# Cross-attention in another order: head 0's scores inside the query product, turning and values alternating with scores

## What is computed

```python
def mem_cross_attn(h, mem, w_q, w_kv, w_o):
    q = _heads(h @ w_q, XA_HEADS).astype(F32)
    k, v = jnp.split(mem @ w_kv, 2, axis=-1)
    k = _heads(k, XA_HEADS).astype(F32)
    v = _heads(v, XA_HEADS).astype(F32)
    p = jax.nn.softmax(jnp.einsum('bhtd,bhmd->bhtm', q, k) * (XA_HD ** -0.5), axis=-1)
    o = jnp.einsum('bhtm,bhmd->bhtd', p, v).astype(h.dtype)
    return _merge(o) @ w_o
...
h = layer_norm(DN_ALPHA * h + mem_cross_attn(...), ln_g[layer, 1], ln_b[layer, 1])
```

## Time and profile before

| | |
|---|---|
| median of 3 runs | 2856.29 us (2851.35 to 2857.38) |
| profiled execution, its own time | 2854.78 us |
| its span, first to last instruction | 2853.1 us |
| mean granted clock of TensorE | 0.965 |
| TensorE busy | 2600.0 us, 91% |
| VectorE busy | 1352.4 us, 47% |
| ScalarE busy | 1072.4 us, 38% |
| share of TensorE in the chain that ended last | 72% |

### The profile page before, as it was taken

One profiled execution on the slowest core, in us unless ns is written; L12 is line 12 of the kernel. 1 busy time (PEld: TensorE's weight loads), 2 busy tenths in 40 slices (PEclk: granted clock), 3 DMA queues, 4 the chain that ended last, 5 costly groups with the idle time before them and its releaser, 6 DMA issues.

```text
span 2853.1 us, 35119 instructions
## 1 busy us (share of the span) xinstructions
PE 2600.0 (91%) x13316; PEld 2107.0 (74%) x13316; DVE 1352.4 (47%) x1869; ACT 1072.4 (38%) x1569; POOL 206.3 (7%) x249
## 2 busy tenths in 40 slices
PE   6978789788999988988899999999997888999999
PEld 5855578567887877776468888888875666788887
DVE  5764377567764355423554333235525544433323
ACT  2235422223454134434644333234424554433322
POOL 1101111001000010000201000001001111100000
PEclk8989989899999999999999999999989999999999
DMA  7730174424323222221012222323310000223232
GB/s 247 265 117 1 47 249 147 162 73 163 118 89 110 96 62 74 88 74 59 1 38 89 89 90 93 103 89 105 104 55 15 22 15 7 67 90 102 90 100 83
DMA packets 178691, 263.21 MB, mean 92 GB/s; under 512 B 8232, under 2 KB 127904, under 8 KB 178592
## 3 DMA queue, kind: packets, MB, share of 16 engines
q1 hardware_dynamic: 156608, 194.00, 20.9%
q0 software_dynamic: 15232, 58.72, 5.9%
q10 hardware_dynamic: 6752, 9.09, 0.9%
HBM read 255.51 MB, written 2.10 MB: 90 GB/s over the span
## 4 chain that ended last, share of the span: by engine, by line
PE 72%; DVE 12%; ACT 7%; issue 5%; POOL 3%; DMA 1%; DVEq 0%; ACTq 0%; SPq 0%; POOLq 0%
PE ps L689 20%; PE ps L691 19%; PE ps L690 19%; PE ps L1281 2%; DVE wlo L2087 2%; PE ps L916 2%; ACT decay L1875 1%; PE ps L958 1%; DVE macc L2104 1%; PE ps L1386 1%; ACT pnt_h L1986 1%; DVE pnt_l L2091 1%; DVE nst L2608 1%; POOL diag L2867 1%; PE ps L1201 1%
## 5 line engine op out<-in xcount | busy, mean ns | idle before, releaser
L2087 DVE TENSOR_TENSOR wlo<-raw,whi 128x2048 fp32r<-128x2048 f32 x180 | 412.1, 2290 | 729.2 <-ACT whi L1506 729.0
L689 PE MATMUL ps<-acth,wlo 128*128 128x512 f32 (+1 forms) x1888 | 703.4, 373 | 24.1 <-DVE actl L2091 12.6
L691 PE MATMUL ps<-acth,whi 128*128 128x512 f32 (+1 forms) x1888 | 696.6, 369 | 0.0
L690 PE MATMUL ps<-actl,whi 128*128 128x512 f32 (+1 forms) x1888 | 696.5, 369 | 0.0
L1506 ACT ACTIVATE whi<-raw 128x2048 fp32r<-128x2048 f32 x180 | 343.6, 1910 | 585.5 <-PE ps L691 585.5
L689 PEld LDWEIGHTS ps<-acth,wlo 128*128 128x128 f32 x1888 | 358.1, 190 | 87.9 <-DVE actl L2091 15.1
L690 PEld LDWEIGHTS ps<-actl,whi 128*128 128x128 f32 x1888 | 358.1, 190 | 60.1 <-issue 1.2
L691 PEld LDWEIGHTS ps<-acth,whi 128*128 128x128 f32 x1888 | 357.4, 189 | 59.8
L689 PE MATMUL ps<-whi,hid_l 128*128 128x512 f32 x528 | 207.9, 394 | 5.2 <-DVE conv_t L2315 3.4
L690 PE MATMUL ps<-wlo,hid_h 128*128 128x512 f32 x528 | 206.2, 390 | 0.0
L691 PE MATMUL ps<-whi,hid_h 128*128 128x512 f32 x528 | 206.0, 390 | 0.0
(11 more groups left out here) (329 smaller groups left out, 3690.9 us busy)
## 6 DMA issues: line engine op xcount, KB each, us to landing
mraw<-in_mod_w POOLq DMA_DIRECT2D x48, 1024.0 KB, 5.5
raw<-in_ffn_w_in SPq DMA_DIRECT2D x44, 1024.0 KB, 4.9
raw<-in_ffn_up SPq DMA_DIRECT2D x22, 1024.0 KB, 4.9
raw<-in_ssm_w_in SPq DMA_DIRECT2D x20, 1024.0 KB, 5.1
raw<-in_ffn_w_out SPq DMA_DIRECT2D x20, 1024.0 KB, 4.9
raw<-in_sb_win SPq DMA_DIRECT2D x12, 1024.0 KB, 5.0
raw<-in_ffn_down SPq DMA_DIRECT2D x10, 1024.0 KB, 4.9
raw<-in_xa_wkv SPq DMA_DIRECT2D x8, 1024.0 KB, 5.1
```

The costliest lines, as they stand in the source:

```text
L689: nc.tensor.matmul(o, ll, rh, start=start, stop=False, skip_group_check=True)
L690: nc.tensor.matmul(o, lh, rl, start=False, stop=False, skip_group_check=True)
L691: return nc.tensor.matmul(o, lh, rh, start=False, stop=stop, skip_group_check=True)
L2087: nc.vector.tensor_tensor(wlo[:, slot, :], raw[:, slot, :], whi[:, slot, :].bitcast(F32), ALU.subtract) \
```

## The change

Head 0's scores are issued inside the second query pair, behind its first two banks, into banks 4 and 5. ACT makes head 0's exponentials right after the split of slot 0, ahead of the copies of query banks 2 and 3; DVE makes head 0's maxima after that split and normalises after the second two modulation units, ahead of the split of slot 1. The pair is written out instead of being a loop of one turn.

In `cross_attention`, `banks_out` and `turns_out` no longer stand in front. Scores of head 1 wait for banks 2 and 3 one by one, and the wait for the modulation store (`turns_out`) stands before the values of head 0. The order on TensorE becomes: turning 0, scores 1, values 0, scores 2, turning 1, scores 3, turning 2, values 1, turning 3, values 2, values 3. The score banks of the heads are 4, 2, 0 and 2. `pxt` has two buffers, the second where the memory input lay. ACT and DVE have orders of their own to match. The output product waits for `heads_free` 4 before its first unit and 8 before its second, in place of 8 before both.

```diff
@@ -317,7 +317,7 @@
     vx = place("vx", [P, MB, D], at=o); o += 8192
     qx = place("qx", [P, KC, SEQ], at=o); o += 16384
     px = place("px", [P, 2, TB, MEM], at=o); o += 8192
-    pxt = place("pxt", [P, MB, SEQ], at=o); o += 4096
+    pxt = [place("pxt0", [P, MB, SEQ], at=o), place("pxt1", [P, MB, SEQ], at=ARENA)]; o += 4096
     o = ARENA
@@ -360,6 +360,8 @@
     w2k = place("w2k", [P, 2, 2, HD], at=WIDE + 7168)
     cst2 = place("cst2", [P, 4, TB * 4 * QG], at=WIDE + 7168)
     kcmp = place("kcmp", [P, KV, CMP], at=SUFFIX)
+    SCORE_BANK = (4, 2, 0, 2)
     T_STRIPS = {3: 0, 2: 512, 0: 896, 1: 1024}
@@ -1023,46 +1025,61 @@
             pe.wait_ge(o_free, 2 + KC)
             turns(o_free, KC)
+        def head_scores(hd):
+            if hd == 0:
+                pe.wait_ge(turned_free, turns.seen["turned_free"] + 4)
+            for t in range(TB):
+                bank = SCORE_BANK[hd] + t // 2
+                if t % 2 == 0:
+                    if hd == 1:
+                        pe.wait_ge(bank_free, turns.seen["bank_free"] + bank + 1)
+                    if hd == 3:
+                        pe.wait_ge(probs, 8)
+                for c in range(2):
+                    last = nc.tensor.matmul(ps[:, bank, MEM * (t % 2):MEM * (t % 2) + MEM],
+                                            qx[:, 2 * hd + c, P * t:P * t + P], kx[:, 2 * hd + c, :],
+                                            start=t % 2 == 0 and c == 0, stop=c == 1, skip_group_check=True)
+                if t % 2:
+                    last.then_inc(scores, 1)
+        def head_turn(hd):
+            pe.wait_ge(probs_normed, hd + 1)
+            if hd:
+                pe.wait_ge(probs_copied, 2 * hd)
+            for m in range(MB):
+                for t in range(TB):
+                    last = nc.tensor.transpose(ps[:, 4 + m, P * t:P * t + P], px[:, hd % 2, t, P * m:P * m + P],
+                                               ident[:])
+                last.then_inc(probs_turned, 1)
+        def head_values(hd):
+            pe.wait_ge(probs_copied, 2 * hd + 2)
+            if hd == 0:
+                turns_out()
+            for c in range(2):
+                if hd:
+                    pe.wait_ge(heads_free, 2 * hd - 1 + c)
+                for m in range(MB):
+                    last = nc.tensor.matmul(ps[:, 6 + c, :], vx[:, m, 256 * hd + P * c:256 * hd + P * c + P],
+                                            pxt[hd % 2][:, m, :], start=m == 0, stop=m == MB - 1)
+                last.then_inc(heads_out, 1)
         def cross_attention():
-            banks_out()
-            turns_out()
-            def head_scores(hd):
-                for t in range(TB):
-                    bank = 2 * (hd % 2) + t // 2
-                    if t % 2 == 0 and hd >= 2:
-                        pe.wait_ge(probs, 4 * (hd - 1))
-                    for c in range(2):
-                        last = nc.tensor.matmul(ps[:, bank, MEM * (t % 2):MEM * (t % 2) + MEM],
-                                                qx[:, 2 * hd + c, P * t:P * t + P], kx[:, 2 * hd + c, :],
-                                                start=t % 2 == 0 and c == 0, stop=c == 1, skip_group_check=True)
-                    if t % 2:
-                        last.then_inc(scores, 1)
-            head_scores(0)
-            for hd in range(XA_HEADS):
-                if hd + 1 < XA_HEADS:
-                    head_scores(hd + 1)
-                pe.wait_ge(probs_normed, hd + 1)
-                if hd:
-                    pe.wait_ge(probs_copied, 2 * hd)
-                for m in range(MB):
-                    for t in range(TB):
-                        last = nc.tensor.transpose(ps[:, 4 + m, P * t:P * t + P], px[:, hd % 2, t, P * m:P * m + P],
-                                                   ident[:])
-                    last.then_inc(probs_turned, 1)
-                for c in range(2):
-                    pe.wait_ge(probs_copied, 2 * hd + 2)
-                    if hd:
-                        pe.wait_ge(heads_free, 2 * hd - 1 + c)
-                    for m in range(MB):
-                        last = nc.tensor.matmul(ps[:, 6 + c, :], vx[:, m, 256 * hd + P * c:256 * hd + P * c + P],
-                                                pxt[:, m, :], start=m == 0, stop=m == MB - 1)
-                    last.then_inc(heads_out, 1)
-            pe.wait_ge(heads_free, 8)
+            head_turn(0)
+            head_scores(1)
+            head_values(0)
+            head_scores(2)
+            head_turn(1)
+            head_scores(3)
+            head_turn(2)
+            head_values(1)
+            head_turn(3)
+            head_values(2)
+            head_values(3)
         def gate_rows_of():
@@ -1453,10 +1470,14 @@
         banks_out()
         token_product(acth, actl, KC, h_sum, summed, mods=4)
         first_pair(h_sum, summed, mods=4)
-        feature_pairs(1, acth, actl, mods=4)
+        banks_out()
+        feature_turn(acth, actl, behind={(0, 1): lambda: head_scores(0)})
+        mod_columns(4)
+        mods_behind[0] += 1
         cross_attention()
         banks_out()
-        token_product(acth, actl, KC, h_sum, summed, mods=4)
+        token_product(acth, actl, KC, h_sum, summed, mods=4,
+                      before_unit=lambda u: pe.wait_ge(heads_free, 4 * u + 4))
         first_pair(h_sum, summed, conv_done, mods=2)
         feature_pairs(3, acth, actl, free=conv_done, mods=2, out=False)
         feature_pairs(FC // 2 - 4, acth, actl, free=conv_done)
@@ -1672,27 +1693,55 @@
                     for u in range(2):
                         weights(pair, u)
+        def exps(hd):
+            act.wait_ge(score_max, hd + 1)
+            if hd >= 2:
+                act.wait_ge(probs_turned, 2 * hd - 2)
+            for t in range(TB):
+                nc.scalar.activation(px[:, hd % 2, t, :],
+                                     ps[:, SCORE_BANK[hd] + t // 2, MEM * (t % 2):MEM * (t % 2) + MEM], ACT.Exp,
+                                     bias=small[:, 4 * (hd % 2) + t:4 * (hd % 2) + t + 1],
+                                     accum_out=small[:, 8 + 4 * (hd % 2) + t:9 + 4 * (hd % 2) + t]) \
+                    .then_inc(probs, 1)
+        def query_pairs():
+            feature_copies(1, qx, 1.0 / 16)
+            for u in range(2):
+                for j in range(2):
+                    act.wait_ge(marks, turns(marks))
+                    nc.scalar.activation(qx[:, 4 + 2 * u + j, :], ps[:, 2 * u + j, :], ACT.Copy, scale=1.0 / 16) \
+                        .then_inc(bank_free, 1)
+                split(u)
+                if u == 0:
+                    exps(0)
         def cross_attention():
...
+            def turned_probs(hd):
                 for m in range(MB):
                     act.wait_ge(probs_turned, 2 * hd + m + 1)
...
+                    if hd >= 2:
+                        act.wait_ge(heads_out, 2 * hd - 2)
+                    nc.scalar.activation(pxt[hd % 2][:, m, :], ps[:, 4 + m, :], ACT.Copy).then_inc(probs_copied, 1)
+            def high(hd):
                 for c in range(2):
                     act.wait_ge(heads_out, 2 * hd + c + 1)
                     nc.scalar.activation(acth[:, 2 * hd + c, :], ps[:, 6 + c, :], ACT.Copy).then_inc(evac_hi, 1)
+            turned_probs(0)
+            exps(1)
+            high(0)
+            turned_probs(1)
+            exps(2)
+            exps(3)
+            turned_probs(2)
+            high(1)
+            turned_probs(3)
+            high(2)
+            high(3)
         def conv_ffn():
             turns(h_ready, 2 * TB)
@@ -2024,7 +2073,7 @@
         summed_blocks(KC)
         load_gb(1)
-        feature_copies(2, qx, 1.0 / 16)
+        query_pairs()
         cross_attention()
         summed_blocks(KC)
         conv_ffn()
@@ -2264,36 +2313,55 @@
                     dve.wait_ge(evac_hi, turns(evac_hi))
                     lo_part(actl[:, pair - 1, :], ps[:, 7, :], acth[:, pair - 1, :]).then_inc(o_free, 1)
+        def maxima(hd):
+            b = 4 * (hd % 2)
+            for k in range(2):
+                dve.wait_ge(scores, 2 * hd + k + 1)
+                last = nc.vector.tensor_reduce(small[:, 16 + b + 2 * k:18 + b + 2 * k],
+                                               ps[:, SCORE_BANK[hd] + k, :].rearrange("p (t m) -> p t m", t=2),
+                                               AX.X, ALU.max)
+            last.then_inc(dve_step, 1)
+            dve.wait_ge(dve_step, turns(dve_step))
+            nc.vector.tensor_scalar(small[:, b:b + 4], small[:, 16 + b:20 + b], -1.0, None, ALU.mult) \
+                .then_inc(score_max, 1)
+        def normalise(hd):
+            b = 4 * (hd % 2)
+            dve.wait_ge(probs, 4 * hd + 4)
+            nc.vector.reciprocal(small[:, 24 + b:28 + b], small[:, 8 + b:12 + b]).then_inc(dve_step, 1)
+            dve.wait_ge(dve_step, turns(dve_step))
+            nc.vector.tensor_tensor(px[:, hd % 2, :, :], px[:, hd % 2, :, :],
```

(72 more changed lines are left out.)

## The result

The changed kernel takes 2834.01 us (median of 4 executions, 2832.95 to 2838.32) against 2856.43 us before, so 22.4 us less by the medians. The measured ratio of the two kernels is 0.9933, 95% interval 0.9918 to 0.9947. The profiled execution, 2838.32 us with a span of 2836.7, was the longest of the four.

A forecast was written before the change was run, and what follows sets the result against it. TensorE bounds the 61.49 us stage by idle gaps and a lowered clock: 17.4 + 8.9 - 0.7 = 25.6 us, about 26 after corrections, so 2856.29 - 26 = 2830.3 us; range 2825 to 2839.

The forecast's parts named there:

- Rival A: Cross-attention stage: clock still falls in one or two stretches, 1.7 to 3.4 us off the gain, some 2833; chance 0.15.
- B: Cross-attention stage: chains of heads 2 and 3 stay unhidden behind in-order ACT and DVE; gain 16.5 us, some 2840; chance 0.08.
- The clock loss: Old stage, query product to output product: TensorE partly at 1.2 GHz after idle gaps, costing 8.94 us.
- within 4 us each time: Argument against a slower result from a lasting low clock: scores and values brought the clock back within 4 us.
- The schedule: Stage in new order, reckoned group by group at full-clock prices: output product starts at 567.1 instead of 592.43, 25.3 us.
- The size of the stage: Query product to output product: stage shortened by 26 us, between 24 and 27.
- the overlap of groups that follow without a wait: TensorE groups in the stage: nine joins overlap by 0.16 us, 1.4 us in all, half of it counted.
- The early scores: Head 0's scores inside the query product: 3.62 us moved, zero by itself; maxima, exponentials and normalising run under TensorE's multiplying.
- The wait for the modulation sum: Moved before head 0's values: turning 0 and scores 1 give 1.5 us of cover; without it 3.35 us again.
- Everything behind moves forward as a block: Everything behind the stage hangs on TensorE's marks and moves forward together, so the stage's gain is kept.
- zero for the added code: Unrolled query loop: 96 matmuls of code added, bounded by at most a 3.35 us gap, taken as zero.
- rival D: Behind the stage: gain given back by mod units or a weight load; partial, 2845 to 2856; chance 0.04.

The follow-up runs named there:

- order alone: Changed kernel, but head 0's scores stand behind the query product, ahead of head 1's; 2840.21 us, ratio 0.9942 to the kernel before.
- before, 16 writes: Kernel before plus 16 one-column VectorE writes in idle time behind the cross-attention, moving later code; 2851.94 us, ratio 0.9984.
- gaps filled with transposes: Kernel before plus unused transposes in TensorE's gaps, 28 behind the query product and 16 before each turning; 2846.00 us, ratio 0.9973.
- columns late: Changed kernel with ten VectorE writes, modulation columns moved off the path between query pairs, fourth modulation unit behind head 1's maxima; 2820.36 us, ratio 0.9868.
- wait in front, 10 writes: Changed kernel with ten VectorE writes, the modulation-sum wait moved from head 0's values to before head 1's scores; 2833.10 us, ratio 0.9931.
- changed, 10 writes: Changed kernel plus ten one-column VectorE writes in idle time behind the cross-attention; 2828.84 us, ratio 0.9916 to the kernel before.
- one buffer, 10 writes: Changed kernel with ten VectorE writes, all heads sharing one `pxt` buffer for turned weights; 2839.01 us, ratio 0.9926 to the kernel before.
- gaps filled with matmuls: Kernel before plus unused matmuls in TensorE's gaps, 14 behind the query product and 8 before each turning; 2851.65 us, ratio 1.0003.
- changed, once more: Changed kernel run a second time, unaltered; 2831.91 us, ratio 0.9912 to the kernel before.
- early scores alone: Kernel before with only head 0's scores moved inside the query product, old order and waits kept; 2866.53 us against 2853.66, ratio 1.0040.
- before, 6 writes: Kernel before plus six one-column VectorE writes in idle time behind the cross-attention, moving later code; 2861.34 us, ratio 1.0045.

## Why the prediction was right, and where it was not

The time, 2834.0 us, lies in the range of 2825 to 2839, 3.7 us above the forecast of 2830.3. That closeness is in part luck: two errors of opposite sign hide in it. The own range of the sum was 2826 to 2834, and the wider one was opened for rivals A and B, of which neither came.

- **The clock loss** was said to be 8.94 us; filling the gaps alone gave 9.0. Right, and shown, for the execution that was read. In the profiles with six and sixteen writes the same gaps lost 4.8 and 6.5 us, so 8.94 was no fixed price. That the clock came back "within 4 us each time" was misread as well: at the scores of heads 0 and 1 the loss of 2.58 us is 5.2 us at half clock.
- **The schedule.** Forecast waits before turnings 2 and 3 of 0.5 and 0.2 us, measured 0.57 and 0.31; modulation sum 1.5 us in time, in fact 1.1 (it ends at 540.96, values 0 start at 542.03); the early normalising 1.6 us before it is needed, with no wait there. Right.
- **The size of the stage.** Forecast 26 us, measured 27.8. The mis-sized term is the overlap of groups that follow without a wait: I took 0.7 us of 1.4. In the trace every join gives its 0.16; that is 0.6 of the 1.8. Another 0.6 is that groups which follow without a wait have shorter rows (values 3.60 instead of 3.70 us), and the first output matmul starts 0.56 us before the row of values 3 ends. The sign for "right" in the prediction, a stage of 32 to 34 us, was missed for the same reason: it took 30.28.
- **The early scores** I called zero by themselves and useful through their cover. In the stage the cover is worth 3.6 us with the new order. Without it nothing is shown: 1.5 us less, with the same idle time, lies within the 4 us by which the old stage varies. The order is nearly all of the stage's gain; of the 21.8 us of the total it alone gave 13.5.
- **The wait for the modulation sum**: 1.5 us of cover, and 3.35 us if it is gone. Put in front, behind turning 0, it cost 2.27 us and another 1.8 through the clock, which I had not added.
- **Rival A** (the clock falls in the new order) did not come: 1.00 in all three profiles of the changed kernel's stage, and with the order alone. It was close, however. The same thin work followed by a wait of 2.27 us was enough.
- **"Everything behind moves forward as a block"**, and zero for the added code, failed. In the profile 9.8 us came back there, as slower matmuls; by the medians it is less: a stage gain of 23.6 to 27.8 us against 22.4 in the total leaves 1 to 5 us. It is rival D in a form that I had not thought of: not a late load, but more time at the lower clock, in part at least through code on VectorE that moved by six instructions. The 96 matmuls of added code do not exist: the query pair was a loop of one turn, and TensorE's program has 8328 instructions instead of 8334.

What is shown: a shift by six makes the pause and makes the kernel before slower by a ratio of 1.0045 (8.4 us by the medians); a shift by sixteen does neither. What is not shown: that the pause is the whole cause. In their profiles the kernel with matmuls in the gaps lost 10.1 us behind the stage without any pause, the one with a single buffer 6.4 us. Common to all profiles of 2267 us and more is that TensorE ran longer at 1.2 GHz in the convolution and in the attention: by the granted clock 34 to 44 us instead of 31 between 400 and 700 us behind the stage, and 55 to 61 us instead of 44 between 1450 and 1800. A profile shows one execution; the last column says how far that one lay from the median of its kernel's runs:

| kernel | pause | behind the stage, us | TensorE busy there, us | profiled execution less median, us |
|---|---|---|---|---|
| before | no | 2260.7 | 2104.6 | -1.6 |
| before, 16 writes | no | 2260.3 | 2104.4 | -0.7 |
| gaps filled with transposes | no | 2260.4 | 2104.5 | +0.7 |
| columns late | no | 2259.8 | 2104.2 | -1.0 |
| wait in front, 10 writes | no | 2261.4 | 2105.9 | -0.7 |
| changed, 10 writes | no | 2262.7 | 2107.7 | +4.2 |
| one buffer, 10 writes | no | 2267.1 | 2112.2 | +2.6 |
| gaps filled with matmuls | no | 2270.7 | 2117.7 | +9.3 |
| changed | yes | 2270.5 | 2116.0 | +4.3 |
| changed, once more | yes | 2269.4 | 2114.3 | +4.4 |
| order alone | yes | 2277.2 | 2121.9 | +6.3 |
| early scores alone | yes | 2276.5 | 2121.3 | +2.4 |
| before, 6 writes | yes | 2263.3 | 2107.5 | -10.0 |

Take the last column off the third (an estimate, as if the whole difference lay behind the stage, which it need not): then the five profiles with the pause come to 2265.1 to 2274.1 us there and the eight without it to 2258.6 to 2264.5. So the kernel with matmuls, whose profile is an unusually long execution, is a weaker case against the pause than it looks. All the same, this is agreement and no proof, and in the changed kernel itself the total times do not tell the pause's share.

My reading, which is not shown, is that in those stages a small shift, from a pause or from another moment of arrival, decides whether the clock falls. The old stage varied in the same way, by 4 us with its waits unchanged. Which moments are good ones stays open.

## What to carry to other kernels

A chain over three engines, repeated per head, is best run two heads deep: values of one head and scores of the next give the cover for turning and normalising. Price each idle gap of TensorE twice, once for its length and once for what the clock costs the matmuls behind it, here 9.0 us on top of 17.4 in one execution and 5 to 6.5 in others: the first price is fixed, the second is not, so take it from more than one profile. And compare the untouched stages of the two profiles too: a change can give back there a part of what it won, and a few harmless instructions more or less help to see whether the place of the code is behind it. Before an effect of some microseconds is read from one profile, look where that execution lies among the kernel's others.

## What the runs showed of the hardware that I had not expected

- Six short instructions added ahead of a loop on VectorE put a pause of 0.36 us into its first turn, and ten more took it away again.
- Transposes of 128 x 128 in the gaps (16 in 1.91 us) kept TensorE's clock at 1.00, as matmuls did.
- The same waits cost a different amount of clock: with 17.4 to 17.5 us of idle time the old stage took 61.5, 61.4, 59.0 and 57.3 us in four executions, at a mean clock of 0.83 to 0.91.
- Two profiles of an unchanged kernel can agree behind the stage (2260.67 and 2260.3 us before, 2270.45 and 2269.44 after) though its other executions are up to 8.5 us shorter (2827.76 to 2836.29 us after, without any edit).
